# Column pieces for one weight pair, a feature-major sample and small norm weight loads in a hybrid retention and HGRN2 step on 8 cores

## The chip, the cores and the metric

The kernel runs on the 8 cores of one Trainium2 chip, one prompt stream and two sample streams on each, with no exchange between cores. A core has five engines with queues of their own: TensorE (PE), VectorE (DVE), ScalarE (ACT), GpSimd (POOL) and SyncE (SP, which here only issues transfers), and 16 DMA engines that all queues share. The metric is the device time of the slowest core in microseconds.

## The reference, cut to what matters

Per stream: a norm, one input projection into eight segments of 512 columns, two recurrences, and an output projection behind a second norm.

```python
h = _rmsnorm(x, g_pre)
u = jnp.einsum('btd,de->bte', h, w_in)            # 1024 -> 4096
rq, rk, rv, rg, hq, hf, hi, hg = jnp.split(u, cuts.tolist(), axis=-1)
# retention: rotary on rq, rk; o = (q k^T * decay mask) v + (q S) * cross_decay; S = decay * S + (k * k_decay)^T v
# HGRN2: f = lb + (1 - lb) * sigmoid(hf); the same form, with a decay per feature from f; hi are its values
o = jnp.concatenate([jax.nn.silu(rg) * _merge(_head_norm(o_r)), jax.nn.silu(hg) * _merge(_head_norm(o_h))], axis=-1)
y = jnp.einsum('bte,ed->btd', o, w_out)           # 1024 -> 1024
return x + _rmsnorm(y, g_post), S_ret, S_hg
```

The prompt has 2048 frames per core and a state that starts at zero; the sample has 2 x 16 frames with states that are read and written.

## The kernel before, in words

The prompt is worked in 4 blocks of 512 tokens, each in 4 tiles of 128. The sample is a fifth block with one tile of 48 rows (its streams at rows 0 to 15 and 32 to 47). `Wi` and `Wo` stay in on-chip memory as bf16. They are loaded once, by POOL's software queue, which turns f32 into bf16 on the way. The loop at L602 issues 12 pieces, all in the first 12 us: the first 1024 columns (segments 0 and 1, retention q and k) in four pieces of two contraction chunks, then columns 1024, 2048, 3072 (segments 2 and 3, 4 and 5, 6 and 7) and `Wo`, each in two pieces of four chunks. Segments 2 and 6 are the values of the two branches, 3 and 7 their gates, 4 and 5 HGRN2's q and forget.

The stages: `stage_A` (L649) loads 128 rows of x, makes their norm with `gpre` on DVE (L680) and turns them feature-major into `xT`, in blocks 0 and 1 by PE transposes (L694). The loads for block 1 wait for the last piece of segments 4 and 5 (L667). `stage_B_hg` (L754) makes HGRN2's q and k per head, from feature-major projections of 512 tokens (`proj_fm`, matmul L715). `stage_B_ret` (L797) makes the rotary q and k, and `stage_C` (L841) values and gates, from token-major projections (`proj_tm`, matmul L732: 128 tokens held, 512 columns of `Wi` streamed, 8 matmuls for a group). `stage_D` does the recurrences of a tile (scores L896, outputs L928 and L933, state L945), `stage_E` (L974) the output projection (L1010), the norm with `gpost` and the residual. `rot` holds rotary tables, `tkT` per-token factors that also scale the retention values (L847).

The order on each engine is written by a planner: every operation is recorded with what it reads and writes (`Sched.op`), costs come from `estimate_costs`, transfers from the little model `Net`, and `list_schedule` picks by start time and priority (longest path, plus a `boost`, plus seeded noise, L224). `slack` (L1133) is added to SP's landings. Each engine then runs its list in order, waiting on semaphores. Where the planner foresees PE idle, `add_fillers` puts dummy matmuls on the identity (L1132): before 16 us one per 60 ns of the gap, later 6 at a time (L397).

The norm weights come as [128, 1024] f32 arrays that the host has repeated over the partitions: `gpre` (L619) among the first loads, `gpost` (L621) behind the last piece of segments 6 and 7.

## Time and profile before

| | us |
|---|---|
| median of 3 runs | 378.24 (378.22 to 398.82) |
| profiled execution | 378.07 |
| its span on the slowest core, core 3 | 376.5 |
| its spans on the other cores | 373.7 to 375.7 |
| PE busy / DVE / POOL / ACT on core 3 | 357.6 / 234.8 / 218.5 / 183.5 |

The span is the time from a core's first to its last instruction; the device time has 1.6 us more around it. Times in the views are counted from the span's start. A matmul's record ends when its result has drained, so records overlap; the distance between starts tells the rate.

### The profile page before, as it was taken

What the parts mean: (1) busy time and instruction counts of PE and PEld (TensorE: products, weight loads), DVE (VectorE), ACT (ScalarE), POOL (GpSimd) and SP (SyncE); (2) the same over time, 40 slices, a digit from 0 to 9 for tenths busy, and PEclk for the clock granted to TensorE, in tenths of its full rate; (3) what the DMA queues carried; (4) which work ended last, traced back from release to release, by engine and by line L of the source; (5) the groups of instructions that cost most, each with busy time, mean ns of one, the idle gap of its engine ahead of it and who ended that gap; (6) DMA issues with size and microseconds to landing.
All of it is one profiled execution on the core that took longest, in us unless ns stands there. A gap on an engine that the chain in (4) does not pass through costs nothing.

```text
span 376.5 us, 7940 instructions; the slowest of 8 cores (373.7 to 376.5 us)
## 1 busy us (share of the span) xinstructions
PE 357.6 (95%) x2343; PEld 188.3 (50%) x2343; DVE 234.8 (62%) x524; ACT 183.5 (49%) x567; POOL 218.5 (58%) x292
## 2 busy tenths in 40 slices
PE   7789799999999999999999999999999999999992
PEld 8554354445554445454545454545455455545541
DVE  0237454995958868658684858666657466458445
ACT  2251244868858746263636262626262534544651
POOL 8425531775668765848565667375647455454640
PEclk9989799999999999999999999999999999999997
DMA  7999999999521979653958346362393464465407
GB/s 175 208 174 165 176 165 205 238 220 181 100 71 17 264 116 254 146 138 78 144 131 200 67 77 142 105 110 83 69 120 69 123 98 127 76 144 134 170 9 190
DMA packets 60619, 51.56 MB, mean 137 GB/s; under 512 B 41632, under 2 KB 48832, under 8 KB 60576
## 3 DMA queue, kind: packets, MB, share of 16 engines
q1 hardware_dynamic: 53104, 32.69, 35.5%
q0 software_dynamic: 7472, 18.35, 32.6%
q8 instruction: 20, 0.33, 0.4%
q14 instruction: 23, 0.19, 0.2%
HBM read 41.73 MB, written 10.09 MB: 138 GB/s over the span
## 4 chain that ended last, share of the span: by engine, by line
PE 78%; DMA 10%; DVE 4%; POOL 3%; ACT 2%; issue 2%; DVEq 0%; POOLq 0%; ACTq 0%
PE bank L732 44%; PE bank L715 15%; PE bank L1010 12%; DMA Wi<-w_in 10%; PE bank L928 2%; PE bank L933 2%; PE bank L945 1%; PE bank L896 1%; ACT og L956 1%; POOL Wi L604 1%; POOL rsq L963 1%; DVE fR L786 1%; PE bank L997 1%; DVE Sst L950 1%; DVE xs L950 1%
## 5 line engine op out<-in xcount | busy, mean ns | idle before, releaser
L732 PE MATMUL bank<-Wi,xT 128*128 128x512 bf16 (+1 forms) x816 | 190.5, 383 | 4.3 <-DMA Wi<-w_in 3.2
L732 PEld LDWEIGHTS bank<-Wi,xT 128*128 128x128 bf16 (+1 forms) x816 | 78.1, 99 | 91.2 <-issue 9.2
L966 DVE SCALAR_TENSOR_TENSOR og<-bank,rsq,gate 128x128 bf16<-128x128 f32 (+1 forms) x136 | 38.8, 343 | 39.9 <-POOL rsq L963 36.5
L1010 PE MATMUL bank<-Wo,ogT 128*128 128x512 bf16 (+1 forms) x272 | 62.1, 379 | 0.2
L715 PE MATMUL bank<-xT,Wi 128*128 128x512 bf16 (+1 forms) x320 | 61.9, 340 | 0.4 <-DVE AT L904 0.3
L885 POOL TENSOR_TENSOR Sst<-Sst,decS 128x512 f32<-128x512 f32 x30 | 32.1, 1078 | 18.4 <-DVE Sst L950 13.0
L715 PEld LDWEIGHTS bank<-xT,Wi 128*128 128x128 bf16 x320 | 26.7, 97 | 31.3 <-issue 3.4
L1010 PEld LDWEIGHTS bank<-Wo,ogT 128*128 128x128 bf16 (+1 forms) x272 | 25.9, 98 | 29.7 <-issue 0.8
L963 POOL TENSOR_TENSOR rsq<-ssq,mhalf 128x4 f32<-128x4 f32 (+1 forms) x34 | 34.5, 1018 | 4.6 <-POOL ssq L960 0.4
L782 POOL TENSOR_TENSOR KTh<-fG 128x512 bf16<-128x512 f32 (+1 forms) x20 | 17.5, 877 | 33.4 <-DVE fG L774 31.7
L956 ACT ACTIVATE og<-bank 128x128 bf16<-128x128 f32 (+1 forms) x136 | 35.6, 287 | 1.7 <-PE bank L933 1.5
L774 DVE TENSOR_TENSOR_SCAN fG<-bank,zer 128x128 f32<-128x128 f32 (+1 forms) x72 | 23.1, 378 | 18.0 <-ACT bank L769 17.6
L855 ACT ACTIVATE gate<-bank 128x512 bf16<-128x512 f32 (+1 forms) x34 | 20.3, 598 | 27.9 <-PE bank L732 27.9
L820 POOL TENSOR_TENSOR Ktr<-tA,tB 128x512 bf16<-128x512 f32 (+1 forms) x17 | 23.1, 1361 | 17.6 <-DVE tB L811 12.4
L1014 ACT ACTIVATE og<-bank 128x512 bf16<-128x512 f32 (+1 forms) x34 | 20.5, 602 | 25.2 <-PE bank L1010 23.3
L889 ACT ACTIVATE Sb<-Sst 128x512 bf16<-128x512 f32 x30 | 19.0, 633 | 27.1 <-POOL Sst L885 21.0
L956 ACT ACTIVATION_READ_ACCUMULATOR og<-bank 128x1 f32 (+1 forms) x136 | 29.7, 219 | 0.0
L786 DVE TENSOR_TENSOR_SCAN fR<-bank,inv,zer 128x128 f32<-128x128 f32 (+1 forms) x72 | 27.4, 439 | 2.5 <-DVE inv L778 0.7
L680 DVE SCALAR_TENSOR_TENSOR xbf<-xs,rsx,gpre 128x1024 bf16<-128x1024 f32 (+1 forms) x13 | 16.6, 1280 | 17.2 <-POOL rsx L677 17.2
L792 POOL TENSOR_TENSOR QTh<-fQ,fR 128x512 bf16<-128x512 f32 (+1 forms) x20 | 22.2, 1109 | 8.7 <-DVE fR L786 3.6
L950 DVE TENSOR_TENSOR Sst<-bank,Sst 128x512 f32<-128x512 f32 x30 | 20.3, 684 | 11.0 <-PE bank L945 6.5
L1028 DVE SCALAR_TENSOR_TENSOR xr<-bank,rs,gpost 128x512 f32<-128x512 f32 x30 | 21.6, 744 | 8.0 <-POOL rs L1024 8.0
(99 smaller groups left out, 460.6 us busy)
## 6 DMA issues: line engine op xcount, KB each, us to landing
xr<-xp POOLq DMA_DIRECT2D x15, 512.0 KB, 6.0
yp<-xr SPq DMA_DIRECT2D x15, 512.0 KB, 3.3
xs<-xp SPq DMA_DIRECT2D x12, 512.0 KB, 6.6
Wi<-w_in POOLq DMA_DIRECT2D x6, 1024.0 KB, 47.0
xr<-xp SPq DMA_DIRECT2D x5, 512.0 KB, 14.1
Wi<-w_in POOLq DMA_DIRECT2D x4, 512.0 KB, 20.3
Wo<-w_out POOLq DMA_DIRECT2D x2, 1024.0 KB, 80.1
rot<-rot_p SPq DMA_DIRECT2D x16, 96.0 KB, 6.4
```

The costliest lines, as they stand in the source:

```text
L715: ins = e.matmul(pb(v)[:, 0:nt], lhsT=Wi[:, kc, col0:col0 + 128], rhs=k.xT[:, kc, 0:nt], start=(kc == 0), stop=(kc == 7))
L732: ins = e.matmul(pb(v)[0:L, :], lhsT=k.xT[:, kc, j * 128:j * 128 + L], rhs=Wi[:, kc, seg * 512:(seg + 1) * 512], start=(kc == 0), stop=(kc ...
L774: S.op(DVE, lambda e, c=c: e.tensor_tensor_scan(out=G[:, c, rsl(cl - 1, cl)], data0=pb(v)[:, rsl(c * st_ + cl - 1, cl)], data1=zer[:, 0:cl ...
L786: S.op(DVE, lambda e, c=c: e.tensor_tensor_scan(out=pack(R)[:, c, :], data0=pb(v)[:, c * st_:c * st_ + cl], data1=zer[:, 0:cl], initial=IV ...
L792: S.op(POOL, lambda e: e.tensor_tensor(out=tok(k.QT[:, h, :]), in0=pack(SQ), in1=pack(R), op=ALU.mult), reads=["fQ", ("fR", f)] + [("fR", ...
L820: S.op(POOL, lambda e, ts=ts, dst=dst: e.tensor_tensor(out=dst[0:L, :], in0=tA[ts][0:L, :], in1=tB[ts][0:L, :], op=ALU.add), reads=[("tA", ...
L885: S.op(POOL, lambda e, Sst=Sst, cc=cc, g=g, gsl=gsl: e.tensor_tensor(out=Sst[:, gsl].rearrange("p (h e) -> p h e", h=4), in0=Sst[:, gsl].r ...
L950: S.op(DVE, lambda e, vd=vd, Sst=Sst, gsl=gsl: e.tensor_tensor(out=Sst[:, gsl], in0=pb(vd)[:, :], in1=Sst[:, gsl], op=ALU.add), reads=[vd, ...
L956: S.op(ACT, lambda e, q_=q_, h=h, vo=vo: e.activation(out=ogs[vs][0:L, h * 128:(h + 1) * 128], in_=pb(vo)[0:L, q_ * 128:(q_ + 1) * 128], f ...
L963: S.op(POOL, lambda e, gq=gq, g=g: e.tensor_tensor(out=rsq[vs][0:L, gq], in0=ssq[vs][0:L, gq], in1=mhalf[0:L, 0:4], op=ALU.pow), reads=[(" ...
L966: S.op(DVE, lambda e, q_=q_, h=h, vo=vo: e.scalar_tensor_tensor(out=ogs[vs][0:L, h * 128:(h + 1) * 128], in0=pb(vo)[0:L, q_ * 128:(q_ + 1) ...
L1010: ins = e.matmul(pb(y)[0:L, :], lhsT=ogT[:, kc, 0:L], rhs=Wo[:, kc, n * 512:(n + 1) * 512], start=(kc == 0), stop=(kc == 7))
```

## The change

Six things change. The second pair of weights (columns 1024 to 2047) is loaded as two pieces of 512 columns with the whole contraction each, segment 2 first, instead of two halves of the contraction over 1024 columns. The norm weights are loaded as [8, 128], 4 KB each; they are split into three bf16 parts, whose sum is spread over all partitions by matmuls against selection matrices and copied from PSUM into `gpre` and `gpost`. The scratch for it is `AT`, `Sst_p` and `ogT`, which are not yet in use. The sample's values and gates are projected feature-major (the weights held, 48 tokens streamed), brought to token-major by PE transposes. Its retention values get their factor from a new table `tkF`, loaded by SP after the scores of the last prompt tile. The late dummy bursts fill six tenths of a planned wait, at least 6 matmuls. The planner's `slack` goes from 3000 to 2000 ns and its noise gets another seed, which changes the whole order; it also charges POOL's transfers of 512 columns 13% more bytes.

```diff
@@ estimate_costs
+                        if e == POOL and name == "dma_start" and out.shape[-1] == 512:
+                            nbytes = int(nbytes * 1.13)
@@ add_fillers
-                    put(burst, {dep_op} | set(bk[2]), bk[1])
-                    for d in reversed(chain[1:]):
-                        put(burst, {dep_op, d} | set(bk[2]), bk[1])
+                    steps = chain[:0:-1]
+                    at = [prev_fin] + [done_at(d) for d in steps] + [o["t_start"]]
+                    for q, d in enumerate([None] + steps):
+                        cnt = max(burst, int(0.6 * (at[q + 1] - at[q]) / fdur))
+                        put(cnt, {dep_op} | set(bk[2]) | (set() if d is None else {d}), bk[1])
@@ build_nc
-    g_pre = din("g_pre", [128, 1024])
-    g_post = din("g_post", [128, 1024])
+    g_pre = din("g_pre", [8, 128])
+    g_post = din("g_post", [8, 128])
...
-            for k0 in range(0, 8, kn):
-                wid = S.op(POOL, lambda e, src=src, dst=dst, c0=c0, k0=k0, kn=kn: e.dma_start(out=dst[:, k0:k0 + kn, c0:c0 + 1024],
-                                                                                             in_=src[:, k0:k0 + kn, c0:c0 + 1024]),
...
+            halves = c0 in (1024,) and nm == "Wi"
+            pieces = [(c, 512, 0, 8) for c in ((c0 + 512, c0) if c0 in () else (c0, c0 + 512))] if halves else [(c0, 1024, k0, kn) for k0 in range(0, 8, kn)]
+            for c1, cw_, k0, kn_ in pieces:
+                wid = S.op(POOL, lambda e, src=src, dst=dst, c1=c1, k0=k0, kn_=kn_, cw_=cw_: e.dma_start(
+                    out=dst[:, k0:k0 + kn_, c1:c1 + cw_], in_=src[:, k0:k0 + kn_, c1:c1 + cw_]),
...
-        gid = S.op(SP, lambda e: e.dma_start(out=gpre[:], in_=g_pre), writes=["gpre"], dma_key="gpre")
-        S.ops[gid]["boost"] = 19.5e6
-        late_dma.append(S.op(SP, lambda e: e.dma_start(out=gpost[:], in_=g_post), writes=["gpost"], dma_key="gpost"))
+        sel, g8, res, part = AT[0:8, :, :], Sst_p[0:8, 0:256], Sst_p[0:8, 256:512], ogT
+        for v, src in enumerate((g_pre, g_post)):
+            S.op(SP, lambda e, v=v, src=src: e.dma_start(out=g8[:, v * 128:(v + 1) * 128], in_=src), writes=[("g8", v)], dma_key=("g8", v))
+        S.op(DVE, lambda e: e.tensor_copy(out=sel, in_=ident[0:8, 0:8].unsqueeze(2).to_broadcast([8, 8, 128])),
...
+        S.op(ACT, lambda e: e.activation(out=p2[0], in_=g8, func=AF.Copy), reads=G8, writes=["ogT"])
+        S.op(DVE, lambda e: e.tensor_tensor(out=res, in0=g8, in1=p2[0], op=ALU.subtract), reads=G8 + ["ogT"], writes=["S0"])
+        S.op(ACT, lambda e: e.activation(out=p2[1], in_=res, func=AF.Copy), reads=["S0"], writes=["ogT"])
+        S.op(DVE, lambda e: e.tensor_tensor(out=p2[2], in0=res, in1=p2[1], op=ALU.subtract), reads=["S0", "ogT"], writes=["ogT"])
+        for v, dst, key in ((0, gpre, "gpre"), (1, gpost, "gpost")):
+            for n in range(2):
...
+                    for q in range(4):
+                        for i in range(3):
+                            ins = e.matmul(pb(T)[:, q * 128:(q + 1) * 128], lhsT=sel[:, n * 4 + q, :], rhs=part[0:8, 2 * i + v, :],
+                                           start=(i == 0), stop=(i == 2))
...
+            if v == 0:
+                for i, o in enumerate(S.ops[n0:]):
+                    o["boost"] = 25e6 - 1e4 * i
...
+        tkf_load = lambda: S.op(SP, lambda e: e.dma_start(out=tkF[:], in_=tkf), writes=["tkF"], dma_key="tkF", deps=[sc0[0]])
@@ stage_C
+            if k.sample:
+                for n, (seg, kind, off) in enumerate(((2, "v", 0), (6, "v", 512), (3, "g", 0), (7, "g", 512))):
...
+                        for c in range(4):
+                            for kc in range(8):
+                                ins = e.matmul(pb(v)[:, c * L:(c + 1) * L], lhsT=Wi[:, kc, seg * 512 + c * 128:seg * 512 + (c + 1) * 128],
+                                               rhs=k.xT[:, kc, 0:L], start=(kc == 0), stop=(kc == 7))
...
+                    if seg == 2:
+                        S.op(DVE, lambda e, v=v, n=n: e.tensor_tensor(out=vgT[:, n, :], in0=pb(v)[:, 0:4 * L], in1=tkF[:, :], op=ALU.mult),
+                             reads=[v, "tkF"], writes=[("vgT", n)])
+                    else:
+                        S.op(ACT, lambda e, v=v, n=n, kind=kind: e.activation(out=vgT[:, n, :], in_=pb(v)[:, 0:4 * L],
+                                                                             func=AF.Copy if kind == "v" else AF.Silu),
...
+                        for c in range(4):
+                            ins = e.transpose(out=pbb(T)[0:L, c * 128:(c + 1) * 128], in_=vgT[:, n, c * L:(c + 1) * L], identity=ident[:])
...
+                    S.op(ACT, lambda e, T=T, dst=dst, off=off: e.activation(out=dst[0:L, off:off + 512], in_=pbb(T)[0:L, 0:512], func=AF.Copy),
+                         reads=[T], writes=[(nm, sl, off)])
+                return
@@ the last lines of build_nc
-        S.slack = 3000.0
-        S.jitter = (10, 500.0)
+        S.slack = 2000.0
+        S.jitter = [(9, 500.0, 0.0, 1.0)]
```

## Rows read from the trace of the kernel before

**Rows 1.** The page's busy shares, core 3.

```profile
PE 357.6 (95%) x2343; PEld 188.3 (50%) x2343; DVE 234.8 (62%) x524; ACT 183.5 (49%) x567; POOL 218.5 (58%) x292
```

**Rows 2.** The chain of waits in order of time, core 3: start, us, what.

```profile
5.84 37.70 DMA Wi<-w_in
```

**Rows 3.** Span and mean granted clock of three of the cores.

```profile
core 2: 373.7 us, clock 0.993
core 3: 376.5 us, clock 0.981
...
core 5: 375.7 us, clock 0.980
```

**Rows 4.** PE's timeline, core 3: start, us, engine, line, operation, [idle before].

```profile
39.43 0.49 PE L1132 MATMUL bank<-ident 128*128 128x128 bf16 x6 [0.36 <-DVE tA L807]
...
43.78 5.83 PE L732 MATMUL bank<-Wi,xT 128*128 128x512 bf16 x16 [0.68 <-DMA Wi<-w_in]
...
60.31 5.34 PE L715 MATMUL bank<-xT,Wi 128*128 128x512 bf16 x24
65.50 1.89 PE L732 MATMUL bank<-Wi,xT 128*128 128x512 bf16 x8
```

**Rows 5.** PE's timelines of core 2 (two rows), then core 5 (one).

```profile
42.75 3.61 PE L732 MATMUL bank<-Wi,xT 128*128 128x512 bf16 x16 [0.54 <-DMA Wi<-w_in]
...
57.07 5.34 PE L715 MATMUL bank<-xT,Wi 128*128 128x512 bf16 x24
...
59.37 5.34 PE L715 MATMUL bank<-xT,Wi 128*128 128x512 bf16 x24
```

**Rows 6.** Windows, core 3: length, busy PE, PEld, DVE, ACT, POOL, clock, DMA, GB/s.

```profile
60.31:360.00 299.69, 296.93 (x1858) 150.88 (x1856) 201.09 (x456) 160.13 (x510) 185.29 (x238) 1.00 0.63 130
...
349.00:365.00 16.00, 15.99 (x136) 8.13 (x132) 7.63 (x31) 9.74 (x37) 8.47 (x16) 1.00 0.29 99
```

**Rows 7.** SP's queue, cores 2, 3, 5: block 1's loads, released by `Wi`.

```profile
56.90 0.92 SPq L663 DMA_DIRECT2D xs<-xp  x2
...
56.82 0.91 SPq L663 DMA_DIRECT2D xs<-xp  x2
...
58.09 1.08 SPq L663 DMA_DIRECT2D xs<-xp  x2
```

**Rows 8.** Windows of the start, core 3, columns as in rows 6.

```profile
10.00:20.00 10.00, 7.11 (x97) 5.77 (x95) 2.57 (x2) 2.06 (x3) 3.89 (x13) 0.88 1.03 204
...
40.00:50.00 10.00, 7.87 (x39) 4.10 (x40) 3.24 (x6) 1.32 (x2) 3.79 (x4) 0.66 1.07 171
```

**Rows 9.** POOL's weight issues; us to landing of the fourth piece and a table.

```profile
1.98 7.61 POOL L604 DMA_DIRECT2D Wi<-w_in  x10 [0.24 <-issue]
...
Wi<-w_in POOLq DMA_DIRECT2D x1, 512.0 KB, 24.8
...
rot<-rot_s SPq DMA_DIRECT2D x2, 12.0 KB, 2.3
```

**Rows 10.** The page's DMA queues: packets, MB, share of 16 engines.

```profile
q1 hardware_dynamic: 53104, 32.69, 35.5%
```

**Rows 11.** Timelines of DVE and ACT at the start, core 3.

```profile
11.62 1.28 DVE L680 SCALAR_TENSOR_TENSOR xbf<-xs,rsx,gpre 128x1024 bf16<-128x1024 f32 x1 [10.42 <-POOL rsx L677]
...
6.72 0.18 ACT L671 ACTIVATION_READ_ACCUMULATOR gate<-xs 128x1 f32 x1
```

**Rows 12.** PE's timeline on core 1: the first transposes of block 1.

```profile
70.05 0.61 PE L694 MATMUL bank<-ident,xbf 128*128 128x128 bf16 x8 [0.46 <-DVE xbf L680]
```

**Rows 13.** PE's timeline and the chain (last two rows) at the sample, core 3.

```profile
348.23 0.56 PE L715 MATMUL bank<-xT,Wi 128*128 128x48 bf16 x16
348.72 0.27 PE L835 MATMUL bank<-ident,qtm 48*128 48x48 bf16 x4
...
355.51 0.45 PE bank L997 x8
357.45 1.73 PE bank L732 x8
```

More of the change, by code:

```diff
@@ L224, in list_schedule @@
         if self.jitter is not None:
-            noise = np.random.RandomState(self.jitter[0]).uniform(-1.0, 1.0, n) * self.jitter[1]
-            for i in range(n):
-                prio[i] += float(noise[i])
+            for seed_, amp_, a_, b_ in self.jitter:
+                noise = np.random.RandomState(seed_).uniform(-1.0, 1.0, n) * amp_
+                for i in range(int(a_ * n), int(b_ * n)):
+                    prio[i] += float(noise[i])
         XLAT = 110.0
@@ L513, in build_nc @@
     tk = din("tk", [128, 2, 12])
+    tkf = din("tkf", [128, 192])
     gl = din("gl", [128, 2, 4])
@@ L586, in build_nc @@
         late_dma = []
+        vgT = sb("vgT", [128, 4, 4 * LS], BF16)
+        tkF = sb("tkF", [128, 4 * LS], F32)
         warm = sb("warm", [128, 1], F32)
@@ new lines, in build_nc @@
+        S.op(DVE, lambda e: e.tensor_copy(out=sel, in_=ident[0:8, 0:8].unsqueeze(2).to_broadcast([8, 8, 128])),
+             reads=["ident"], writes=[("AT", 0), ("AT", 1)])
+        G8 = [("g8", 0), ("g8", 1)]
+        p2 = [part[0:8, 2 * i:2 * i + 2, :].rearrange("p a b -> p (a b)") for i in range(3)]
+        S.op(ACT, lambda e: e.activation(out=p2[0], in_=g8, func=AF.Copy), reads=G8, writes=["ogT"])
+        S.op(DVE, lambda e: e.tensor_tensor(out=res, in0=g8, in1=p2[0], op=ALU.subtract), reads=G8 + ["ogT"], writes=["S0"])
@@ new lines, in build_nc, with bc @@
+        S.op(ACT, lambda e: e.activation(out=p2[1], in_=res, func=AF.Copy), reads=["S0"], writes=["ogT"])
+        S.op(DVE, lambda e: e.tensor_tensor(out=p2[2], in0=res, in1=p2[1], op=ALU.subtract), reads=["S0", "ogT"], writes=["ogT"])
+        for v, dst, key in ((0, gpre, "gpre"), (1, gpost, "gpost")):
+            for n in range(2):
+                T = S.bank()
+                def bc(e, v=v, n=n, T=T):
+                    ins = None
+                    for q in range(4):
+                        for i in range(3):
+                            ins = e.matmul(pb(T)[:, q * 128:(q + 1) * 128], lhsT=sel[:, n * 4 + q, :], rhs=part[0:8, 2 * i + v, :],
+                                           start=(i == 0), stop=(i == 2))
+                    return ins
+                S.op(PE, bc, reads=["ogT", ("AT", 0), ("AT", 1)], writes=[T])
+                S.op(ACT if n == 0 else DVE, (lambda e, dst=dst, T=T: e.activation(out=dst[:, 0:512], in_=pb(T)[:, :], func=AF.Copy)) if n == 0 else
+                     (lambda e, dst=dst, T=T: e.tensor_copy(out=dst[:, 512:1024], in_=pb(T)[:, :])), reads=[T, "S0"], writes=[(key, n)])
+            if v == 0:
+                for i, o in enumerate(S.ops[n0:]):
+                    o["boost"] = 25e6 - 1e4 * i
@@ L681, in stage_A @@
                                                        in1=gpre[0:L, :], op0=ALU.mult, op1=ALU.mult),
-                 reads=[xkey, ("rsx", sq), "gpre"], writes=[("xbf", slot)])
+                 reads=[xkey, ("rsx", sq), ("gpre", 0), ("gpre", 1)], writes=[("xbf", slot)])
             if i == 3:
@@ L1020, in stage_E @@
                                                                   in1=gpost[0:L, n * 512:(n + 1) * 512], op=ALU.mult),
-                         reads=[y, "gpost"] + yd, writes=yk)
+                         reads=[y, ("gpost", n)] + yd, writes=yk)
             S.op(POOL, lambda e: e.tensor_scalar(out=rs2[0:L, :], in0=ss2[0:L, 0:1], scalar1=ss2[0:L, 1:2], scalar2=EPS,
@@ L1030, in stage_E @@
                                                                     op0=ALU.mult, op1=ALU.mult),
-                         reads=[ybk[n], "rs2", "gpost"], writes=[("xr", slot) if n == 0 else ("xr1", slot)])
+                         reads=[ybk[n], "rs2", ("gpost", n)], writes=[("xr", slot) if n == 0 else ("xr1", slot)])
                 S.op(POOL, lambda e: e.dma_start(out=xr[slot][:], in_=xp[t0:t0 + 128, :], accum_op=ALU.add),
```

23 lines of the change are left out of this document (19 added, 4 removed).

## Prediction

> **What bounds the kernel now.** I read the page's busy shares first. PE is busy 95% of the span, so for most of the run the time is PE's own work [rows 1]. The chain of waits tells where it is not: it runs through `Wi<-w_in` from 5.84 us for 37.7 us, and from 43.78 us through PE's matmuls [rows 2, 4]. In that stretch DMA is full: a share of 1.03 in 10 to 20 us, 1.07 in 40 to 50 [rows 8].
>
> Next the cores, because the time is that of the slowest: core 3 with 376.5 us, against 373.7 for core 2 and 375.7 for core 5 [rows 3]. The PE timelines say where they part. Call H the first L715 matmul, the start of the HGRN2 projections of block 0, which needs the whole third pair of weights (segments 4 and 5). H is 60.31 us on core 3, 57.07 on core 2, 59.37 on core 5 [rows 4, 5]. From H to the end of the span is 376.5 - 60.3 = 316.2, 373.7 - 57.1 = 316.6 and 375.7 - 59.4 = 316.3 us. **So everything behind H takes 316.3 us whichever core it is, and a core's span is H plus that.** PE is idle there for only 299.7 - 296.9 = 2.8 us up to 360 us [rows 6].
>
> What sets H? SP issues block 1's input loads when the last piece of segments 4 and 5 has landed: 56.9 us on core 2, 56.8 on core 3, 58.1 on core 5 [rows 7]. On core 2 H follows that landing by 0.2 us, so it has no slack left. Core 3 is 3.5 us behind it: its PE did little from 38.6 us on (six dummies at a time, waits between: one such burst at 39.43), and the first 16 matmuls on segment 2 took 5.83 us where core 2 took 3.61 [rows 4, 5]. Granted clock in 40 to 50 us: 0.66 on core 3, that is part of the stretch at 1.2 GHz instead of 2.4 [rows 8]. Two bounds therefore stand side by side: the weight stream, and PE's late start on segments 2 and 3.
>
> **The change part by part.**
>
> *Segments 2 and 3 as column pieces.* Before, each piece holds half of the contraction for both, so no group of L732 on them can close until the second lands at 43.5 us. After, values are complete after the first piece. POOL issued ten pieces from 1.98 us on in 7.6 us; the fourth, the last of the first pair, thus near 4.3 us, and it landed 24.8 us later, at 29.1. The next two took 43.5 - 29.1 = 14.4 us [rows 2, 9], so values come about 7 us before 43.5. Four groups of 8 matmuls at 1.73 us (6.9 us) move into a stretch where PE ran dummies. Cores late for H by PE's fault, as core 3, gain until the landing of segments 4 and 5 stops them; a core like 2 gains nothing. Also the eighth group on segments 2 and 3, which core 3 ran at 65.50 behind H [rows 4], goes ahead of H: -1.7 us on the rest.
>
> The price is in the stream: 1,024 rows of 1 KB written instead of 512 of 2 KB in each piece. No row shows that form. From below: the same bytes, nothing. From above: the hardware queue's packets of mean 0.6 KB took 0.355 x 376.5 x 16 / 53,104 = 40 ns each [rows 10], so a fixed part is at most 40 ns; a piece's packet took 14.4 us x 16 / 1,024 = 225 ns; half of the rest plus 40 is 132, twice that 265, +18%, 2.6 us. The diff's own planner line charges 13%; I take that, 1.9 us, being near the upper bound.
>
> *Norm weights.* A 512 KB load of `gpre` leaves the full DMA stretch, one of 4 KB comes. At the 204 to 171 GB/s of the stretches shown [rows 8] it is worth 0.52 MB / 0.204 to 0.171 = 2.6 to 3.1 us; nothing if the other queue does not take up the room. I take 2.7, since DMA is full and the weights go in order behind each other. The new chain (two loads, four small ACT and DVE steps, 48 matmuls of 128 columns, four evictions) must end before the first use of `gpre` at 11.62 us. DVE was idle for 10.42 us ahead of it [rows 11], and PE ran dummies. Priced by ACT's and DVE's small steps, 0.2 to 0.7 us each, it is under 6 us behind the load and hidden; ACT's first Square waits behind it by about 1 us; its result lay ready at 6.9 and was used at 11.62, as POOL was issuing weights, so 1 us is inside that. Uncovered, the delay would hit H only through 5 us of spare time before the landing. The late `gpost` load also goes; nothing on the chain waits for it, so nothing.
>
> So H: 58.1 (slowest landing) - 2.7 + 1.9 + 0.2 = **57.5 us**, bounds 55.2 (3.1 and nothing) and 60.9 (nothing and 2.6).
>
> *Behind H.* Block 1's inputs are loaded only after that same landing, and on core 1 its first transposes at 70.05 waited 0.46 us on DVE's norm [rows 12]. With 1.7 us of filler work gone PE would come there 1.7 + 0.5 us early; it can pull the last two HGRN2 groups forward. 0 to 2.3 us; I take 0.8.
>
> *Longer dummy bursts.* They cover six tenths of a planned wait instead of 0.5 us. PE now waits before H instead of before 43.8. If the clock falls there, the first groups cost what core 3 paid, 5.83 - 3.61 = 2.2 us; else nothing. Core 2 waited as long without a fall, so I take 0.7.
>
> *The sample, feature-major.* A 512-column group on 48 rows is 1.73 us. A group of 8 matmuls of 48 columns runs in 0.24 us (16 from 348.23 to 348.72), so 32 take about 1.0; four transposes of 128 columns 0.22 (8 in 0.45), say 0.25 [rows 13]. Per segment 1.73 - 1.0 - 0.25 = 0.5, four times: -2.0 us; with a quarter more or less time per matmul, 39 or 23 ns, -0.9 or -3.0. PE is busy 15.99 of the 16 us from 349 to 365, so it counts [rows 6]. New evictions go to ACT, busy 9.7 of those 16 us. The new `tkF` load waits on SP for the last prompt tile's scores; behind it stand the sample's rotary loads and the state stores. The sample's retention values wait for it. The scores are among the last prompt work, ahead of the sample's projections at 348 [rows 13], and the 12 KB rotary load lands in 2.3 us [rows 9]: nothing, or one PSUM bank held for some us.
>
> The matmuls of 48 columns start 31 ns apart [rows 13]. The Trainium skill (TensorE: Matmul & The Clock Gate, section "Wait — 56ns, not 53.3ns?") gives about 62 ns for each matmul issued through the sequencer's code and a floor of about 25 ns otherwise. By the first, as an estimate, 32 take 1.98 us, the sample would lose 2.0 us instead of gaining 2.0, and the time would be 377.2; the trace's 31 ns stand near the second.
>
> *Order.* A smaller slack and another noise reorder every engine. PE's idle of 2.8 us is the most that can be won, and I allow as much lost; I take 0.
>
> **Sum.** 57.5 + 316.3 - 1.7 + 0.8 + 0.7 - 2.0 = 371.6 us of span. The profiled run took 378.07 with a span of 376.5, 1.6 outside it: **373.2 us**, 1.3% less. The median of the runs, 378.24, is 0.2 above the profiled one.
>
> **Rivals.**
> 1. *The wait only moves.* H comes early, but PE stands at block 1's first tile (2.3) and the clock falls before H (2.2): 373.2 - 1.5 + 4.5 = 376.2. For it: core 1's wait there, core 3's slow matmuls. Against: core 2 met neither in full.
> 2. *All of it lands.* H at 55.2, no wait, no slow clock, sample -3.0: 55.2 + 316.3 - 1.7 - 3.0 + 1.6 = 368.4. For it: core 2's clock of 0.993. Against: every term at its end.
> 3. *The stream pays per row, not per byte: slower.* The two pieces take twice 14.4 us, H = 58.1 - 2.7 + 14.4 + 0.2 = 70.0, and the time 70.0 + 316.3 - 1.7 - 2.0 + 1.6 = 384.2. It decides when H passes 62.4 with the other terms as I took them, the two pieces 6.8 us (47%) slower. Against: the 40 ns above.
> 4. *In a run of 32, the 48-column matmuls start no closer than those of 128 columns* (8 in 0.45 us [rows 13], 56 ns): 32 take 1.8 us, the sample loses 4 x (1.8 + 0.25 - 1.73) = 1.3 us, and the time is 373.2 + 2.0 + 1.3 = 376.5. Against: 16 of them at 31 ns in a row. The Trainium skill's 62 ns on the page named above would be this rival.
>
> **Numbers.** Forecast with small misses (371 to 375.5) 0.52; rival 1 0.20; rival 2 0.17; rival 3 0.05; rival 4 or an order that loses 2 to 3 us 0.06. Taking in the middle of rivals 1 and 2, the range is 369.5 to 377.5. Two per cent, about what a measurement of this kernel can tell from no change, is 7.6 us: below 370.7 is rival 2 and a little of the forecast, 0.19; above 385.8 only more than rival 3, 0.02; within, 0.79.
>
> **What would show it.** First matmul on segment 2 near 34 to 37 us; H within 0.3 us of the landing of segments 4 and 5 on all cores, at 56.5 to 58.5; full clock behind H; 316.3 less about 3 us from H to the end; the cores' spans closer together than 2.8 us. I am wrong if H is not set by that landing, if the landing moves by more than 2 us, or if PE's idle behind H grows past 3 us.

## The result and the profile after

The changed kernel takes 382.0 and 382.6 us, the one before 378.2 to 378.6 us beside it: a ratio of 1.0104 with a 95% interval of 1.0075 to 1.0133. It is slower by 1.0%, 3.9 us; I had predicted 373.2 us, 1.3% faster, with a range up to 377.5. (Two further executions of the changed kernel, near 441 us, were disturbed and stay out of every comparison.) The profiled execution took 382.6 us, with a span of 381.1 us on its slowest core.

Spans and granted clock of the slowest core and of one of the two fastest, answering to [rows 3]:

```profile
core 1: 381.1 us, clock 0.983
core 2: 377.9 us, clock 0.988
```

The page's busy shares, core 1, answering to [rows 1]:

```profile
PE 360.0 (94%) x2551; PEld 195.6 (51%) x2551; DVE 238.0 (62%) x529; ACT 187.3 (49%) x575; POOL 217.9 (57%) x292
```

The cut at H, the first matmul on segment 4 (now L752), still works. SP's queue of core 1 at block 1's loads, which the landing of segments 4 and 5 releases:

```profile
58.81 0.80 SPq L700 DMA_DIRECT2D xs<-xp  x2
```

PE's timeline of core 1 around H:

```profile
55.22 2.56 PE L1201 MATMUL bank<-ident 128*128 128x128 bf16 x43
58.88 5.34 PE L752 MATMUL bank<-xT,Wi 128*128 128x512 bf16 x24 [1.10 <-DMA Wi<-w_in]
64.06 1.00 PE L1201 MATMUL bank<-ident 128*128 128x128 bf16 x15
66.03 5.34 PE L752 MATMUL bank<-xT,Wi 128*128 128x512 bf16 x24 [0.97 <-DVE fR L823]
72.11 0.61 PE L731 MATMUL bank<-ident,xbf 128*128 128x128 bf16 x8 [0.75 <-DVE xbf L717]
72.56 0.89 PE L1201 MATMUL bank<-ident 128*128 128x128 bf16 x13
75.09 3.45 PE L752 MATMUL bank<-xT,Wi 128*128 128x512 bf16 x8 [1.64 <-POOL QTh L829]
```

H is 58.88 us, 0.07 us behind the landing; over the eight cores it is 57.6 to 59.2, within 0.7 us of the landing on each, where before it was 57.1 to 60.3. So the landing sets H now, as I said, but the latest H came down by 1.1 us only; my sum had it at 57.5. **The loss is behind H:** 319.9 to 322.2 us instead of 316.1 to 316.9. On core 1 it is 322.2, 5.9 us more than before, where my sum had 314.1. Of the 9.5 us of span that the sum missed on this core (381.1 against 371.6), 1.4 are ahead of H and 8.1 behind it. Three windows of core 1 (columns as in [rows 6]): from H to 360 us, the 15 us behind H, and the end up to the sample's output projection.

```profile
58.88:360.00 301.12, 294.05 (x1975) 153.03 (x1975) 201.15 (x455) 159.36 (x503) 181.70 (x235) 0.99 0.62 129
58.88:73.88 15.00, 12.85 (x84) 6.62 (x84) 9.97 (x25) 8.39 (x16) 5.10 (x8) 1.00 1.06 222
340.00:370.07 30.07, 25.91 (x361) 16.27 (x360) 14.33 (x49) 17.26 (x70) 13.63 (x26) 0.94 0.39 102
```

The last two stretches on core 3 of the kernel before:

```profile
60.31:75.31 15.00, 14.87 (x78) 6.87 (x77) 11.06 (x29) 10.32 (x18) 7.36 (x9) 1.00 1.05 235
340.00:365.79 25.79, 24.90 (x240) 13.63 (x238) 15.84 (x51) 14.85 (x63) 13.43 (x24) 1.00 0.36 106
```

PE idles 2.15 us instead of 0.13 right behind H, and 4.16 instead of 0.89 at the end. Idle time understates the waits behind H, because dummies count as busy: with the 15 and 13 dummies of the timeline, PE does no work of the block for 1.97 us from 64.06 and for 2.53 us from 72.56. Before, no dummies ran behind H. The chain of waits of core 1 says on what, behind H: DVE's scans and POOL's product of the HGRN2 stage, one behind the other.

```profile
64.27 1.53 DVE fR L823 x4
...
65.85 1.38 DVE fG L811 x4
...
67.61 1.62 DVE fR L823 x4
...
71.89 1.37 DVE fG L811 x4
...
73.67 1.28 POOL QTh L829
...
75.09 3.45 PE bank L752 x8
```

The last group on segments 2 and 3, which PE ran between these stages before ([rows 4], at 65.50), is done ahead of H now; nothing is left to fill in. The last row is a second loss: 8 matmuls in 3.45 us, half the rate, at a granted clock of 0.52 from 75.0 to 78.4 us. That is core 1 alone; the other seven have 1.00 there. Core 7 lost as much one group earlier: behind 1.98 us of idle ahead of H its first 24 matmuls took 7.03 us, at a clock of 0.74 from 57.5 to 64 us.

The end, PE's timeline of core 1:

```profile
351.12 0.96 PE L889 MATMUL bank<-xT,Wi 128*128 128x48 bf16 x32
351.92 0.36 PE L752 MATMUL bank<-xT,Wi 128*128 128x48 bf16 x8
...
361.02 5.31 PE L1078 MATMUL bank<-Wo,ogT 128*128 128x512 bf16 x16
...
368.56 0.38 PE L1013 MATMUL bank<-V,Kth 16*128 16x128 bf16 x4 [1.32 <-ACT Kth L989]
...
370.07 3.61 PE L1078 MATMUL bank<-Wo,ogT 128*48 128x512 bf16 x16 [0.41 <-ACT ogT L1068]
```

The 32 matmuls of 48 columns start within 0.80 us (351.12 to 351.92), even less than my 1.0. But the last prompt tile's output projection, 16 matmuls, takes 5.31 us where it took 3.63: it runs at 1.2 GHz for most of its length. That is so on seven of the eight cores (5.1 to 5.7 us). The two output projections stand 9.0 us apart (361.02 and 370.07); before it was 5.4.

The terms for core 1: idle behind H +2.0, the half-rate group +1.7, idle further on in the first 50 us +0.8, idle at the end +3.3, the slow output projection +1.7, the group moved ahead of H -1.7, the sample's projections -2.2 (four times 1.73 against 3.6 us of matmuls and 1.1 of transposes). That is +5.6, of the 5.9 measured. The sum comes so near by some luck: it leaves out the 1.6 us of dummies behind H, and small terms of the other sign.

### The profile page after: what moved, and what is told of

The parts are those of the page before. It is cut to its first block, busy times and chain, and to the rows that moved or that the text cites. A ratio compares the mean times of both kernels' runs of the same rounds, so it can differ in the third digit from the quotient of the medians.

```text
span 381.1 us, 8388 instructions; the slowest of 8 cores (377.9 to 381.1 us)
## 1 busy us (share of the span) xinstructions
PE 360.0 (94%) x2551; PEld 195.6 (51%) x2551; DVE 238.0 (62%) x529; ACT 187.3 (49%) x575; POOL 217.9 (57%) x292
## 4 chain that ended last, share of the span: by engine, by line
PE 88%; DVE 4%; issue 3%; POOL 2%; ACT 1%; DVEq 0%; another core or an unknown queue 0%; POOLq 0%; ACTq 0%
PE bank L769 42%; PE bank L1078 15%; PE bank L752 14%; PE bank L1201 4%; PE bank L996 2%; PE bank L1001 2%; PE bank L1013 2%; PE bank L964 2%; PE bank L889 1%; PE bank L731 1%; DVE fR L823 1%; PE bank L649 1%; DVE fG L811 1%; POOL rsx L714 1%; PE bank L1065 1%
## 5 line engine op out<-in xcount | busy, mean ns | idle before, releaser
L769 PE MATMUL bank<-Wi,xT 128*128 128x512 bf16 (+1 forms) x784 | 179.5, 379 | 1.1 <-DVE Sst L1018 0.5
L769 PEld LDWEIGHTS bank<-Wi,xT 128*128 128x128 bf16 (+1 forms) x784 | 74.5, 98 | 83.7 <-issue 2.1
L752 PE MATMUL bank<-xT,Wi 128*128 128x512 bf16 (+1 forms) x320 | 64.1, 346 | 4.2 <-POOL QTh L829 1.6
L1078 PE MATMUL bank<-Wo,ogT 128*128 128x512 bf16 (+1 forms) x272 | 64.7, 386 | 0.4 <-ACT ogT L1068 0.4
L752 PEld LDWEIGHTS bank<-xT,Wi 128*128 128x128 bf16 x320 | 27.2, 98 | 34.3 <-issue 7.1
L957 ACT ACTIVATE Sb<-Sst 128x512 bf16<-128x512 f32 x30 | 18.9, 630 | 35.1 <-POOL Sst L953 12.9
L953 POOL TENSOR_TENSOR Sst<-Sst,decS 128x512 f32<-128x512 f32 x30 | 31.1, 1039 | 8.7 <-DVE Sst L1018 8.2
L857 POOL TENSOR_TENSOR qtm<-tA,tB 128x512 bf16<-128x512 f32 (+1 forms) x17 | 22.5, 1322 | 22.3 <-DVE tA L844 13.8
L923 ACT ACTIVATE gate<-bank 128x512 bf16<-128x512 f32 x32 | 19.1, 597 | 30.7 <-PE bank L769 30.6
L819 POOL TENSOR_TENSOR KTh<-fG 128x512 bf16<-128x512 f32 (+1 forms) x20 | 18.5, 927 | 24.2 <-DVE fG L811 24.1
L844 DVE TENSOR_TENSOR tA<-bank,rot 128x512 f32<-128x512 f32 (+1 forms) x34 | 23.1, 682 | 9.3 <-PE bank L769 6.4
L857 POOL TENSOR_TENSOR Ktr<-tA,tB 128x512 bf16<-128x512 f32 (+1 forms) x17 | 21.6, 1269 | 9.3 <-DVE tB L848 5.6
## 6 DMA issues: line engine op xcount, KB each, us to landing
xr<-xp SPq DMA_DIRECT2D x5, 512.0 KB, 14.4
```

The costliest lines, as they stand in the source:

```text
L752: ins = e.matmul(pb(v)[:, 0:nt], lhsT=Wi[:, kc, col0:col0 + 128], rhs=k.xT[:, kc, 0:nt], start=(kc == 0), stop=(kc == 7))
L769: ins = e.matmul(pb(v)[0:L, :], lhsT=k.xT[:, kc, j * 128:j * 128 + L], rhs=Wi[:, kc, seg * 512:(seg + 1) * 512], start=(kc == 0), stop=(kc ...
L844: S.op(DVE, lambda e, v=v, ts=ts, cosb=cosb: e.tensor_tensor(out=tA[ts][0:L, :].rearrange("p (a d) -> p a d", d=64), in0=pb(v)[0:L, :].rea ...
L857: S.op(POOL, lambda e, ts=ts, dst=dst: e.tensor_tensor(out=dst[0:L, :], in0=tA[ts][0:L, :], in1=tB[ts][0:L, :], op=ALU.add), reads=[("tA", ...
L953: S.op(POOL, lambda e, Sst=Sst, cc=cc, g=g, gsl=gsl: e.tensor_tensor(out=Sst[:, gsl].rearrange("p (h e) -> p h e", h=4), in0=Sst[:, gsl].r ...
L1078: ins = e.matmul(pb(y)[0:L, :], lhsT=ogT[:, kc, 0:L], rhs=Wo[:, kc, n * 512:(n + 1) * 512], start=(kc == 0), stop=(kc == 7))
```

## The experiments

The theories were: (A) the new order of all engines costs the time behind H; (B) the feature-major sample costs it; (C) the weights' landing costs it, by the column pieces. Ratios are to the kernel before, with 95% intervals. H and landings come from one profiled execution of each kernel. Some of the expectations below name theories A to D of their own; those are told in the expectation itself and are not the three above.

| kernel | ratio | interval |
|---|---|---|
| before, slack and noise seed of the change | 1.0170 | 1.0118 to 1.0222 |
| before, seed alone | 1.0328 | 1.0304 to 1.0353 |
| before, slack alone | 1.0099 | 1.0080 to 1.0118 |
| changed, slack and seed of before | 1.0187 | 1.0146 to 1.0228 |
| changed, sample token-major | 1.0093 | 1.0060 to 1.0126 |
| changed, no column pieces | 1.0191 | 1.0125 to 1.0256 |
| order held: column pieces | 1.0042 | 1.0020 to 1.0064 |
| order held: norm loads | 0.9995 | 0.9985 to 1.0005 |
| order held: sample feature-major | 1.0049 | 1.0033 to 1.0066 |
| order held: longer bursts | 0.9965 | 0.9950 to 0.9979 |
| order held: norm loads, bursts | 1.0001 | 0.9983 to 1.0019 |
| order held: all four | 1.0078 | 1.0043 to 1.0113 |
| order held: norm loads, chain early | 1.0062 | 1.0039 to 1.0084 |
| the same with bursts | 1.0010 | 0.9995 to 1.0025 |
| order held: all four, chain early | 1.0128 | 1.0105 to 1.0152 |
| the same, sample token-major | 1.0019 | 1.0004 to 1.0035 |
| order held: norm loads, few dummies | 0.9977 | 0.9956 to 0.9998 |
| the same with bursts | 0.9966 | 0.9950 to 0.9983 |

### What an order costs

Four kernels change the planner's two numbers and nothing else. Before with both numbers of the change:

```diff
-        S.slack = 3000.0
-        S.jitter = (10, 500.0)
+        S.slack = 2000.0
+        S.jitter = (9, 500.0)
```

> The kernel before with only the changed kernel's slack of 2000 ns and noise seed 9: same operations, another order. If the order as such costs the 3.7 us by which the changed kernel is slower (382.0 against 378.3), this run takes 381 to 383 us. If the parts of the change cost it (the sample's small matmuls at the end, the HGRN2 stretch with nothing beside it), it stays within 1 us of 378.3.

Before with the seed alone, and with the slack alone (one line of the two each):

> The kernel before, replanned with noise seed 9 instead of 10, slack 3000 ns kept. If the noise alone is worth several us, 381 to 385 us; if the slack is the cause, within 1 us of 378.4.

> The kernel before, replanned with a slack of 2000 ns instead of 3000, noise seed 10 kept. Slack and seed together cost 6.4 us (1.7%). If the slack is the cause (operations planned before their transfers have landed, so that an engine waits in order), 383 to 385 us with the transfers from SP named in the waits; if the noise is, within 1 us of 378.4.

The changed kernel with both numbers of before (the same two lines, backwards):

> The changed kernel with the slack of 3000 ns and noise seed 10 of the kernel before. By the order theory 377 to 379 us. By the theory that the parts cost it, 381 to 383 us, with the stretch from the first HGRN2 projection to the end again near 320 to 322 us instead of 316.3.

The same instructions in another order cost 1.0 to 3.3%, 3.7 to 12.4 us. The seed alone, the worst, leaves the start as it was (landing 56.7 to 57.8, H 56.9 to 60.1) and takes 324.8 to 328.0 us behind H. PE's waits on core 0 (releaser: us in total, times, longest):

```profile
PE bank L1010 <- DVE fR L786: 2.6, 1, 2.6
PE bank L732 <- ACT gate L671: 1.9, 1, 1.9
...
PE bank L997 <- DVE og L966: 1.7, 2, 1.4
PE bank L945 <- ACT Kth L921: 1.7, 2, 1.2
```

The page's busy shares on that core, the slowest:

```profile
PE 361.8 (93%) x2349; PEld 190.8 (49%) x2349; DVE 235.4 (61%) x524; ACT 185.0 (48%) x567; POOL 217.7 (56%) x292
```

No single wait is long. PE stands one to two and a half microseconds at several places for DVE or ACT, and its busy time is 4.2 us more for the same work [rows 1], mostly because some of it runs at a lower clock (0.968 on this core against 0.981 on core 3 before [rows 3]). Theory A is possible, then, and the sizes are larger than any part of the change. The last of the four shows the reverse: the numbers of before are no better for the changed kernel, 1.9% instead of 1.0%. Three of the four lose more than their expectation had at most, and the slack alone lies between its two.

### One part taken out of the changed kernel

The sample token-major:

```diff
-            if k.sample:
+            if False:
                 for n, (seg, kind, off) in enumerate(((2, "v", 0), ...
-                tkf_load()
```

> The changed kernel with the sample's values and gates token-major again, all else as changed. If the sample's form costs the loss behind 340 us (from the last prompt tile's output projection to the sample's 9.1 us instead of 5.4, TensorE at 1.2 GHz in it), this run takes 378 to 379 us and that distance is back at 5 to 6 us. If the loss is in the HGRN2 stretch alone, it stays at 381 to 382.5.

The second pair as two halves of the contraction:

```diff
-            halves = c0 in (1024,) and nm == "Wi"
+            halves = False
```

> The changed kernel with the second pair of weights again as two halves of the contraction over 1024 columns. Column-piece theory: the pair takes 14 us again instead of 16.9, the third pair lands 2 to 3 us earlier (55 to 57 us), block 0's gate group fills the HGRN2 stretch, TensorE's idle time from 60 to 80 us falls from 2.3 to 3.4 us to under 1, and the time is 378 to 379.5. If the pieces are free and the sample is all, it stays at 381.5 to 382.5.

Neither brings the time back. Without the feature-major sample the slow end is gone, as the PE timeline of its core 1 shows (full rate, and 5.9 us apart; the last row is cut off by the end of the view):

```profile
363.14 3.63 PE L1078 MATMUL bank<-Wo,ogT 128*128 128x512 bf16 x16
...
369.04 3.18 PE L1078 MATMUL bank<-Wo,ogT 128*48 128x512 bf16 x14 [0.40 <-ACT ogT L1068]
```

Behind H it takes 1.4 us less (a mean of 319.4 against 320.8), but the landing was up to 60.4 us in this kernel, and the times are 1.0093. Without the pieces the landing comes 1.6 us earlier (a mean of 56.56 against 58.16), and 321.6 to 325.6 us follow. PE's idle in the first 15 us behind H goes down (0.6 to 1.4 us on the eight cores, against 1.0 to 2.4 in the changed kernel), but in the 35 us behind those it is 2.5 to 3.7 us (0.1 to 1.3 in the changed kernel). Each of these kernels is planned anew, so each compares two orders as well as one part; by the section above that alone is worth several microseconds. They decide nothing on the parts.

### The parts with the order held

So I took the planner out. In the following kernels each engine's list of the kernel before is written out and replayed; instructions that a part adds stand at fixed places, the others keep theirs. Dummies are put in by the same rule as before. The traces bear out that the order holds: with dummies left out, every engine's instructions on core 3 come in the order of before, one for one (2,140 matmuls on PE), in the kernels with the pieces alone and with the bursts alone. No replay without any part was run; the one with the norm loads takes 315.9 to 316.8 us behind H, as before, so a cost of the replay itself does not show there.

```diff
-            order = self.list_schedule()
+            order = self.replay(FIXED)
```

One part of the change each, its lines as in the diff above: the column pieces, the norm loads, the sample feature-major (its matmuls where the token-major group stood, transposes and copies right behind), the longer bursts.

> The kernel before with each engine's list of instructions kept as it was; only the second pair of weights is loaded as two column pieces. Order theory: the parts cost little by themselves, and what a part costs is seen only with the order held. The pieces' own price, read from the landing of segments 4 and 5 (58.2 us in the mean of the cores with pieces, 56.6 without): 1.6 us later, so 379.0 to 380.5 us, and from the first HGRN2 projection to the end still 316 us. If the pieces cost nothing, 378 us.

> The kernel before with its order kept; only the norm weights come as 4 KB and are spread on the chip. By the prediction the third weight pair lands 2.7 us earlier and the slowest core gains 1 to 2 us: 376 to 377. By what the run without pieces showed (landing 56.6 against 57.1 in the mean) 0.5 us: 377.5 to 378.3.

> The kernel before with its order kept; only the sample's values and gates are feature-major, each new transpose and copy put right behind the eviction that it follows. By the prediction's sum 2.0 us less: 376.3. By the clock theory (small matmuls and waits for ScalarE let TensorE fall to 1.2 GHz in the last output projections, 5.3 us for 16 matmuls instead of 3.6, and the chain gets longer) 379.5 to 381.5.

> The kernel before with its order kept; only the late dummy bursts fill six tenths of a planned wait. If the slow first matmuls on segment 2 of some cores (5.8 us for 16 instead of 3.6) come from the thin bursts ahead of them, they run at 2.4 GHz on all cores, the slowest core reaches the HGRN2 projections at the weights' landing (57 to 58 us instead of 60.3), and the time is 375.5 to 377. If the bursts do not decide the clock, or hold up work behind them, 378 to 379.

**Column pieces: 0.4% slower.** H is at the landing on every core, and the landing is 57.8 to 60.4 us, a mean of 58.8 instead of 57.1. On the slowest core SP's queue is released by the landing at 60.40 us, and PE's timeline has H there (the row is cut off by the end of the view):

```profile
60.36 1.89 PE L835 MATMUL bank<-xT,Wi 128*128 128x512 bf16 x8 [1.31 <-DMA Wi<-w_in]
```

That is 1.7 us, near the 1.9 that I had charged for the rows of 1 KB, and the PE side gives nothing back: cores whose PE was late are early now, and wait for the stream.

**The sample: 0.5% slower.** The time is that of the expectation's clock theory, but the reason is not: with this order the slow output projection is absent, and 316.8 to 317.2 us follow H on seven cores, 318.9 on one. PE's timeline of core 2, three places where the saved time went:

```profile
343.74 1.67 PE L852 MATMUL bank<-Wi,xT 128*128 128x512 bf16 x7 [0.55 <-DVE fR L906]
...
353.01 0.38 PE L988 MATMUL bank<-ident,vgT 128*48 128x128 bf16 x4 [0.61 <-DVE vgT L977]
...
364.38 0.35 PE L1148 MATMUL bank<-ident,og 48*128 48x48 bf16 x8 [0.73 <-DVE og L1117]
```

PE's idle from 340 us on is 2.6 to 3.1 us instead of 0.9 to 1.3: the recurrences of the sample wait for its values, which now pass through two copies and a transpose. The mean behind H is 317.1 us instead of 316.4, 0.7 of the 1.9 us that the ratio stands for. H itself, up to 61.1 us on one core, is in the time too, and the sample runs long after H; where the rest of the 0.5% comes from stays open.

**Bursts: 0.35% faster,** 376.8 to 377.6 us, between the two expectations, with H 56.8 to 59.3 and the clock at 0.994 to 0.997 on all cores, where before it was down to 0.980 [rows 3]. The place is the wait ahead of segments 2 and 3: from 36 to 48 us the granted clock is 1.00 on all eight cores, where before it was 0.73 to 0.86 on cores 3 to 7.

Then two parts, and all four:

> The kernel before with its order kept, small norm weight loads and longer bursts together. With the norm loads alone the third pair landed 0.5 us earlier in the mean (56.6 against 57.1), but seven cores ran the first matmuls on segment 2 at 1.2 GHz and reached the HGRN2 projections at 59.7 to 60.1. If the bursts keep the clock, that start follows the landing on every core, at 56 to 58 us, and the time is 375.5 to 377. If the two do not add up, 377.4 as with the bursts alone.

> All four parts of the change in the order of the kernel before (each engine's list kept, new instructions put in). If the parts add up, 378.4 + 1.6 - 0.2 + 1.9 - 1.3 = 380.4, 379.5 to 381.5, and the rest of the changed kernel's 382.0 is its order. If the parts disturb each other, 382 or more.

All four with the order of before give 1.0078, the change itself 1.0104, with overlapping intervals; so the change does not pay in the old order either. But the two lose in different places. Replayed, everything behind H takes 317.0 to 317.6 us, a mean of 0.7 more than before, and H is late, 58.5 to 60.9. In the change H is 57.6 to 59.2, and 319.9 to 322.2 us follow. The slowest core of the replay: its span, PE behind H, and the window of 15 us behind H:

```profile
core 5: 377.9 us, clock 0.993
...
60.89 5.34 PE L861 MATMUL bank<-xT,Wi 128*128 128x512 bf16 x24
66.07 1.89 PE L878 MATMUL bank<-Wi,xT 128*128 128x512 bf16 x8
...
60.89:75.89 15.00, 14.86 (x78) 6.91 (x77) 11.09 (x29) 10.32 (x18) 7.32 (x9) 1.00 1.06 232
```

The last group on segments 2 and 3 keeps its place there, at 66.07, and PE idles 0.14 us in the 15 (at most 0.57 on any core) where the change has 2.15 on core 1. **So most of the 3 to 5 us behind H belong to the new order, with the parts' operations in it: in this replay the same operations in the old order don't lose them.** What H loses in the replay is the norm chain's: the first transposes come at 17.1 to 18.1 us on seven cores, and H is 1.6 to 3.4 us behind the landing there; the new order places the chain better (14.8 to 15.3 us). The sum of the single ratios is 1.0051; norm loads and bursts don't add up (1.0001).

### Where the norm loads' gain went

In the two kernels with norm loads and no pieces the landing was 55.4 to 57.5 us but H 59.7 to 60.9 on seven cores of each: PE was late. The first transposes of x came at 17.5 to 17.9 us on seven cores in the norm loads' kernel, 13.0 to 14.0 before. Their chain stood behind dummies on PE, and ACT's first Square behind the chain's copies. The next two place the chain early, without bursts and with them; besides the lines shown, ACT's list has the first Square ahead of the copies, and the model that times the replay lets the two small loads land sooner:

```diff
+                    o["fill_max"] = 30
...
-                        put(int((gap - margin) / fdur), {dep_op} | set(bk[2]), bk[1])
+                        put(min(int((gap - margin) / fdur), o.get("fill_max", 9999)), {dep_op} | set(bk[2]), bk[1])
```

> The order of the kernel before, with the 4 KB norm weight loads, but their chain placed well: 30 dummy matmuls ahead of the spreading matmuls instead of 109, and ACT's first Square ahead of the copies to gpre. Theory A (in the earlier run with the norm loads the gain was eaten because the chain stood behind dummies on PE and ahead of the first Square on ACT, so that the first norm came at 15.2 us instead of 11.6, the first transposes at 17.5 instead of 13.3 and everything of the first pair 3.5 us late): first norm back at 11.6 us, first transposes at 13.3, the third pair's landing at 56.6, the first L715-like matmul (H) between 56.8 and 59, ratio 0.995 to 0.998. Theory B (the small loads are worth nothing to this kernel wherever they stand, since the landing moves by 0.5 us only and PE's slow start decides): H as before, 57 to 60.3, ratio 0.999 to 1.001. Theory C (the chain costs by itself, by more PE work or by its copies): ratio above 1.001.

> As the run with the norm chain placed early, and the longer dummy bursts too. Theory A: the two add up, H within 0.5 us of the landing on all cores, 56.8 to 58, ratio 0.992 to 0.995 (bursts alone were 0.9965). Theory B: nothing on top of the bursts, 0.996 to 0.997. Theory C: worse than the bursts alone, 0.998 to 1.000, as in the earlier run with both.

The first norm was back at 11.5 to 12.5 us, but theory A's times were missed: without bursts the time is theory C's, with them just beyond it (1.0010). The trace shows why. PE's timeline of the kernel with bursts, core 0 (here and on core 2 the last row is cut off by the end of the view):

```profile
10.40 6.52 PE L1311 MATMUL bank<-ident 128*128 128x128 bf16 x87
16.76 0.61 PE L842 MATMUL bank<-ident,xbf 128*128 128x128 bf16 x8
...
59.72 2.10 PE L863 MATMUL bank<-xT,Wi 128*128 128x512 bf16 x9
```

The same on core 2:

```profile
8.01 6.66 PE L1311 MATMUL bank<-ident 128*128 128x128 bf16 x87
14.51 0.61 PE L842 MATMUL bank<-ident,xbf 128*128 128x128 bf16 x8
...
57.45 4.26 PE L863 MATMUL bank<-xT,Wi 128*128 128x512 bf16 x18
```

87 dummies now stood ahead of the transposes, which ran them at 14.4 to 17.9 us. H follows: 59.72 - 16.76 = 42.96, 57.45 - 14.51 = 42.94, and on all eight cores of this kernel 42.94 to 42.97, though the landings were 54.9 to 56.9. (In the kernel with the late chain it is 42.2 us, 59.82 - 17.65 on core 0.) **In this order PE and the engines it waits for need 42 to 43 us from the first transposes to H; H comes no earlier than that, and not before the landing.** Two more kernels therefore cut the dummies:

```diff
-                    o["fill_max"] = 30
+                    o["fill_max"] = 40
...
-                        put(min(int((gap - margin) / fdur), o.get("fill_max", 9999)), ...
+                        put(min(int((gap - margin) / fdur), o.get("fill_max", 50)), ...
```

> As the run with the norm chain placed early, but 40 dummy matmuls ahead of the spreading matmuls and at most 50 between them and the first transposes (there 30 and 87; the first norm was ready at 12.8 us and its transposes stood behind those 87 until 17.2 to 18.8). Theory A (what the norm loads lose is PE's queue of dummies at the start, which run at 95 to 110 ns each where the planner counts 60): first transposes at 12.9 to 13.7 us as before, H 57 to 59, ratio 0.996 to 0.999. Theory D (H is late with the norm loads for another reason): H again 59 to 62 on most cores, ratio 1.000 to 1.006.

> As the run before it, with the longer dummy bursts. Theory A: H within 1 us of the landing, 56.5 to 58.5, ratio 0.993 to 0.9965 (bursts alone 0.9965: at that end the loads themselves are worth nothing). Theory D: 0.998 to 1.002.

With bursts the transposes come at 12.9 to 14.4 us, H is 56.4 to 57.7, and the cores span 372.3 to 374.0 us in the profiled execution. The times are 375.6 to 377.8 us (0.9966), the same as the bursts alone. Without bursts it is 0.9977, inside theory A's range. The dummies are the cause of what the norm loads lost, not the chain's own work; mended, the loads bring about 0.2% alone and nothing on top of the bursts, not the 2.7 us of the prediction. The mean landing is 56.1 to 56.8 us in these four kernels, 0.3 to 1.0 us earlier than before. Last, all four parts with the chain early, and the same without the feature-major sample:

> The order of the kernel before with all four parts, the norm chain placed early. The same four parts with the late chain gave 1.0078. Theory A: the late chain was 1 to 2 us of that, ratio 1.002 to 1.005, H at 57.5 to 59, first norm 11.6 us. Theory B or C (the late chain was hidden there, since the pieces' landing at 58.8 sets H): 1.007 to 1.009.

> As the run with all four parts and the early chain, but the sample token-major as before. If the feature-major sample costs what it cost alone (0.5%), this is 0.4 to 0.6% faster than that run; if its cost came from waits that another order takes up, 0 to 0.2%. In numbers by theory A 0.998 to 1.001, by B or C 1.002 to 1.004.

These still have the 87 dummies. 1.0128 is beyond what any theory expected, and the 1.1% between the two is more than the sample cost alone. In the first, cores 5 and 6 run from 340 to 370 us at a mean clock of 0.89 and 0.83 and take 319.6 and 322.3 us behind H (the other six 317.7 to 318.5); in the second all cores are at 1.00 there. So the slow end of the change does not need the new order. Among all profiled executions one of the last two output projections takes over 5 us only where the sample is feature-major (among them the changed kernel, the one without the pieces and this one with all four), and there not on every core or in every order.

**The best version** is the one with the bursts alone: 377.35 us at the median, faster than the kernel before and the changed one. With the norm loads and few dummies it is the same.

## Why the prediction was wrong, point by point

The largest step that failed is the term for the order: it was put at 0 with bounds of 2.8 us, and the change takes 3.7 us more behind H in the mean than the same parts in the old order (320.8 against 317.1). With it failed the price of emptying the stretch behind H, 0.8 us for a wait in the wrong place, and the 2.0 us of gain for the sample.

- **H is set by the landing of segments 4 and 5, and the column pieces take away PE's late start.** Right: H is within 0.7 us of the landing on all cores, and the first matmul on segment 2 comes at 37.0 us on core 1. No core lost to the half-rate start that core 3 had before; the clock is 1.00 on all eight from 36 to 46 us.
- **Norm loads, -2.7 us of H.** Wrong by size: the mean landing moves 1.0 us at best. The step that failed is pricing the load at the 204 to 171 GB/s of the stretch: it left the other queue, and the weights' queue took up little of its room; the lower bound of nothing was the nearer one. The second half of the term failed too. I called the chain hidden with 5 us to spare; on core 2 there was 0.8 (57.07 - 13.34 - 42.94), because the transposes start PE's own 43 us to H. In the changed kernel they come at 14.8 to 15.3 us instead of 13.0 to 14.0.
- **Pieces, +1.9 us.** Right, 1.7 in the means. But I let the gain on PE's side and this loss end up in one sum over the slowest core (58.1); the slowest landing differs by 0.9 to 1.3 us from one profiled kernel to the next (57.8 to 58.7 in six with the loads of before, 59.1 to 60.4 in three with the pieces).
- **The eighth group ahead of H, -1.7, and a wait of 0.8 behind H.** The direction of the wait was right, the place not. I looked at block 1's first transposes, which waited 0.75 us. The larger waits are on DVE's scans and POOL inside block 0's HGRN2 stage: with all of them PE idles 2.15 us in 15, which takes back all of the 1.7. The prediction asked of the filler work only what it cost PE, not what it hid.
- **Bursts, +0.7 us lost to the clock.** In the change the clock fell ahead of H on one core of eight: core 7 paid 1.7 us (7.03 instead of 5.34 for the first 24 matmuls), core 1, the slowest, nothing. Alone, in the old order, the bursts bring 0.35%; there they keep up the clock on segments 2 and 3, a gain that I had left to the new order.
- **The sample, -2.0 us.** The term of PE was right: 0.80 us for 32 matmuls, 25 ns each. The Trainium skill's page TensorE: Matmul & The Clock Gate (section "Wait — 56ns, not 53.3ns?") has both the floor of about 25 ns and the 62 ns; the trace agrees with the floor. Rival 4 is out. What failed is the step from "PE is busy 15.99 of 16 us" to "so it counts": with PE quicker, it stands waiting for the copies of ACT and DVE and what hangs on them (4.16 us of idle at the end instead of 0.89). Alone the part costs 0.5%; in the change the output projection at half rate adds 1.7 us on core 1.
- **Order, 0 with bounds of 2.8.** The worst step. PE's idle of 2.8 us bounds what an order can win; I used it as a bound on what it can lose, without a reason. Replans of the same instructions lose 3.7 to 12.4 us, and the change loses 3.7 us in the mean behind H that the replay of all four parts in the old order does not. With bounds of that size the range would have held the result.
- **The rivals.** Rival 1, the wait only moves, is nearest in kind, but its 376.2 us had one wait and a slow clock ahead of H; measured are three waits behind H, a wait for the sample, and slow clocks behind H and at the end. Rival 3 has nearly the right time (384.2) for a cause that did not occur: the pieces were 1.7 us slower, not 14.4.
- **What would show it.** I had written that I am wrong if the landing moves by more than 2 us or if PE's idle behind H grows past 3 us. The second is what happened: 7.1 us up to 360 us (301.12 - 294.05), where it was 2.8. Three signs of being right were missed as well: H within 0.3 us of the landing (0.7), H at 56.5 to 58.5 us (57.6 to 59.2), and spans closer together than 2.8 us (3.2).

## What to carry to other kernels

Before you credit parts of a change that lets a planner replan everything, hold each engine's order and price the parts alone; and price the replan from replans of the same instructions, since the idle time that is left bounds a gain and says nothing of a loss. When work is moved out of a stretch, ask what it hid there, not only what it cost. Dummy work that keeps a clock up is a queue like any other: count what stands behind it at the rate that it really runs at.

## What the runs showed that I had not expected

The first dummies on PE take about twice the time of the later ones, although the record gives the full clock. Two windows of the kernel before, core 2 (columns as above): 21 of them in 2 us, then 40.

```profile
2.00:4.00 2.00, 2.00 (x21) 2.00 (x21) 0.00 (x0) 0.77 (x2) 2.00 (x3) 1.00 0.90 279
...
8.00:10.00 2.00, 2.00 (x40) 2.00 (x38) 0.00 (x0) 0.00 (x0) 2.00 (x4) 1.00 0.94 225
```

The planner counts 60 ns for each, so in the changed kernel 95 of them held the norm chain until 9.51 us, whose inputs were ready at 4.86 on core 2:

```profile
1.86 7.72 PE L1201 MATMUL bank<-ident 128*128 128x128 bf16 x95 [1.86 <-POOL mhalf L602]
9.51 2.85 PE L649 MATMUL bank<-ogT,AT 8*128 8x128 bf16 x48
```

And the clock fell behind a stretch in which PE was rarely idle. From 351 to 361 us core 1 of the changed kernel ran 221 short matmuls with PE busy 9.35 of 10 us at a clock of 1.00 (by records whose ends are modelled); in the next 6 us it was 0.72. Without the feature-major sample it stayed at 1.00; there the same stretch of core 1 has 104 matmuls, among them groups of 512 columns. Windows of the changed kernel:

```profile
351.00:361.00 10.00, 9.35 (x221) 7.49 (x219) 4.12 (x18) 6.98 (x23) 4.16 (x9) 1.00 0.48 144
361.00:367.00 6.00, 6.00 (x32) 2.51 (x32) 0.86 (x3) 2.77 (x14) 3.27 (x5) 0.72 0.04 11
```

And of the one with the token-major sample, core 1:

```profile
351.00:361.00 10.00, 10.00 (x104) 5.59 (x102) 4.68 (x19) 5.92 (x19) 5.29 (x10) 1.00 0.30 104
361.00:367.00 6.00, 6.00 (x33) 2.62 (x31) 2.13 (x7) 3.04 (x16) 3.27 (x5) 1.00 0.04 11
```

Why some orders of the feature-major sample escape this, and what makes the order of the kernel before better than its three replans by 4 to 12 us, stays open; a few waits on DVE and ACT are all that the traces show, and no further orders were tried.
